# The order of the products inside a weight chunk: output tile outside, contraction step inside

## The chip, the cores and the metric

The kernel runs on one core of a Trainium2 chip. The metric is the device time of one execution in microseconds; the median of three runs is given. The profile is of one further execution of the same program.

## The reference

Two transformer-like blocks are applied one after the other to 256 tokens of width 2048, in float32. The first takes the tokens through a conditioned norm, a projection to four parts (a state space mixer and dilated attention), an output projection and a gated feed-forward network. The second puts 16 meta tokens ahead of them and applies a feed-forward network, a projection, a pooling mixer and forget-gate attention, an output projection and a third feed-forward network. Cut to the part that matters here, which is the dense products:

```python
proj = h @ w_in                      # 2048 x 4096
y = y * sigmoid(y @ w_glu)           # 1024 x 1024
x = x + gate1 * (mixed @ w_out)      # 2048 x 2048
x = x + gate2 * ((silu(h2 @ w_gate) * (h2 @ w_up)) @ w_down)   # hidden 5632
# the second block: the same kinds of product again,
# h + 0.5 * swiglu(...), u @ w_in_2, mix @ w_out_2, h + 0.5 * swiglu(...)
```

## The kernel before, in words

**Tiling.** Everything lies transposed: features on the 128 partitions, tokens along the free dimension (256 tokens, or 272 with the meta tokens). A weight matrix is read in chunks of 512 rows by 512 columns, 1 MB each, as a tile of 128 partitions x 4 contraction steps (CK = 4) x 512 columns. A chunk feeds four output tiles of 128 features, m = 0 to 3. A group is the chunks that accumulate into the same four output tiles, 4 of them in most stages (cpg), 2 or 3 in a few.

**Precision.** Each float32 product is made of three: the weights are split into a high and a low part, and so are the activations. TensorE computes high weight x high activation (L540), high weight x low activation (L541) and low weight x high activation (L542). So a chunk is 4 steps x 4 tiles x 3 = 48 products, each with a load of 128 x 128 weights ahead of it.

**Order of the work.** SyncE issues the loads into a ring of four raw buffers (`stream`, L388) and waits for the user of the buffer four chunks before. ScalarE splits off the high part into one of two buffers (`split_hi`, L404) when the products of the chunk two before are done (chunk_done). VectorE computes the low part (`split_lo`, L409) and signals lo_ready. TensorE runs `products`: for each chunk it waits once for the group's four PSUM banks if it is the group's first (bank_free), for the activations where they are new, and for lo_ready, and then issues the 48 products. The last of them signals chunk_done. Between chunks VectorE and ScalarE also empty the PSUM banks of the finished group (L742, L796 and others), and there are two sets of four banks, so that one is filled while the other is emptied.

**Where tiles lie.** `out_tile` (above `products`) gives each of the four output tiles a PSUM bank of its own, in the half that the group has. Only in w_in do two tiles of 256 columns share a bank (m // 2), and there only the even tile's first product has the start flag.

**Who calls it.** `products` is used for all dense stages: w_in (with the pieces of the state space mixer between the chunks, `beside`), glu, w_out, the up and down parts of the three feed-forward networks (`ffn_pe`), w_in_2 and w_out_2. There are 496 chunks. Elsewhere, at L1898, the forget gate of the second block is computed with 48 products from weights of 8 columns, all into one tile:

```python
for k in range(KT):
    for w, x in ((wf_hi, act_hi), (wf_hi, act_lo), (wf_lo, act_hi)):
        mm = pe.matmul(ps[0:HEADS, 4, 0:T], w[:, k, :], x[:, k, :], ...
```

Of the kernel before, what the change touches and what calls it, by code (L numbers as in the profile page):

```python
# [35 lines left out]
CK = 4  # L36
# [110 lines left out]
def build(nc, a, out):  # L147
# [4 lines left out]
    with stack:  # L152
# [197 lines left out]
        def loop(eng, start, end, body):  # L350

            if end - start == 1:
                body(start)
            elif end > start:
                with eng.Fori(start, end) as i:
                    body(i)
# [140 lines left out]
        def group_index(p, it, g):  # L497

            return 1 + p.g0 // 2 + g // 2 + it * (p.groups // 2)
# [9 lines left out]
        def out_tile(name, half, m, n):  # L509

            if name == "w_in":
                return ps[:, 2 * half + m // 2, n * (m % 2):n * (m % 2) + n]
            return ps[:, 4 * half + m, 0:n]

        def products(pe, name, hi, lo, cols, ready, norm=None, beside=None):
            p = byname[name]
            n = cols.stop - cols.start
            shared = name == "w_in"

            def body(it, norm=None):  # L520
                for j in range(p.per["S"]):
                    g, c = divmod(j, p.cpg)
                    half = g % 2
                    if norm and j == 3:
                        norm_pe(pe, norm, 4)
                    if norm and j == 4:
                        pe.wait_ge(ms_ready, NORMS.index(norm) + 1)
                    if beside:
                        beside(it * p.per["S"] + j)
                    if c == 0:  # L530
                        pe.wait_ge(bank_free[half], group_index(p, it, g))
                    if ready(c) is not None:
                        pe.wait_ge(*ready(c))
                    pe.wait_ge(lo_ready, p.before["S"] + it * p.per["S"] + j + 1)
                    for t in range(CK):
                        k = CK * c + t
                        for m in range(4):
                            o = out_tile(name, half, m, n)
                            whi, wlo = w_hi[j % 2][:, t, P * m:P * m + P], w_lo[j % 2][:, t, P * m:P * m + P]
                            pe.matmul(o, whi, hi[:, k, cols], start=(k == 0 and not (shared and m % 2)), stop=False)  # L540
                            pe.matmul(o, whi, lo[:, k, cols], start=False, stop=False)  # L541
                            mm = pe.matmul(o, wlo, hi[:, k, cols], start=False, stop=(k == CK * p.cpg - 1 and not (shared and m % 2 == 0)))  # L542
                    mm.then_inc(chunk_done, 1)

            if norm:
                body(0, norm)
            for it in range(p.iters if beside else 0):
                body(it)
            loop(pe, 1 if norm else p.iters if beside else 0, p.iters, body)


# [11 lines left out]
        def norm_pe(pe, name, bank_=0):  # L563

            i = NORMS.index(name)
            for g in range(QUADS):
                pe.wait_ge(ssq_ready, QUADS * i + g + 1)
                mm = pe.matmul(ps[:, bank_, 0:T], ones, ssq[:, g, :], start=(g == 0), stop=(g == QUADS - 1))  # L568
            mm.then_inc(ssq_sum, 1)
# [1421 lines left out]
```

## Time and profile before

| | |
|---|---|
| median of 3 runs | 3419.1 us (3419.04 to 3423.09) |
| profiled execution, its own time | 3418.91 us |
| its span, first to last instruction | 3416.8 us |
| mean granted TensorE clock | 0.944 of full speed |
| TensorE products busy | 3190.7 us, 93% |
| VectorE busy | 1925.2 us, 56% |
| ScalarE busy | 1209.9 us, 35% |
| GpSimd busy | 198.0 us, 6% |
| read from HBM | 626.16 MB, mean 184 GB/s |

A matmul's row in the timeline has its start and its duration. Successive matmuls overlap, so the spacing of their starts, and not the duration, says how fast TensorE goes. PE is TensorE's matmuls, PEld its weight loads, DVE is VectorE, ACT ScalarE, POOL GpSimd, SP SyncE; q behind a name is that engine's queue of instructions. ps is the tile of all eight PSUM banks.

### The profile page before, as it was taken

The numbers are of one execution on the slowest core, as the hardware profiler recorded it, in microseconds if no ns is written. First come the engines' busy times: TensorE is split into PE (matmuls) and PEld (weight loads), VectorE is DVE, ScalarE is ACT, GpSimd is POOL, SyncE is SP. The second block draws the span as 40 slices with busy tenths as digits, with TensorE's granted clock in tenths as the row PEclk, the third lists the DMA queues.
The fourth block names the chain that finished last, engine by engine and source line by source line (L and its number), as shares of the span: only waits on it lengthen the run. The fifth ranks groups of instructions, "written<-read, shape, count | busy, mean of one in ns | idle before, by whom it ended". The sixth has DMA issues, their size and how long they took to land. (4 is left out here: it accounts for less than half of the span.)

```text
span 3416.8 us, 57672 instructions
## 1 busy us (share of the span) xinstructions
PE 3190.7 (93%) x25282; PEld 3105.7 (91%) x25282; DVE 1925.2 (56%) x1800; ACT 1209.9 (35%) x1067; POOL 198.0 (6%) x194
## 2 busy tenths in 40 slices
PE   3499758799999999999999999999899999999999
PEld 3499648799999999999999999999659999999999
DVE  7888597867444444654445445654335554455454
ACT  2264423333233333433333333433324433333333
POOL 3434120000000000000000000021000000000000
PEclk6699859899999999999999999999859999999999
DMA  9765357577555555555555555588205555555553
GB/s 328 243 204 191 129 185 271 210 270 268 174 185 185 188 189 187 185 170 177 173 173 172 178 175 176 173 173 171 79 1 178 181 187 188 182 191 187 185 184 136
DMA packets 328689, 630.26 MB, mean 184 GB/s; under 512 B 22452, under 2 KB 24008, under 8 KB 328280
## 3 DMA queue, kind: packets, MB, share of 16 engines
q1 hardware_dynamic: 317512, 624.79, 55.6%
q10 hardware_dynamic: 11040, 3.51, 0.5%
q8 instruction: 103, 1.69, 0.2%
q14 instruction: 34, 0.28, 0.0%
HBM read 626.16 MB, written 2.10 MB: 184 GB/s over the span
## 5 line engine op out<-in xcount | busy, mean ns | idle before, releaser
L409 DVE TENSOR_TENSOR w_lo<-raw,w_hi 128x2048 fp32r<-128x2048 f32 x496 | 1139.6, 2298 | 1266.7 <-ACT w_hi L404 1266.5
L404 ACT ACTIVATE w_hi<-raw 128x2048 fp32r<-128x2048 f32 x496 | 949.8, 1915 | 1803.5 <-PE ps L542 1755.1
L540 PE MATMUL ps<-act_hi,w_hi 128*128 128x256 f32 (+1 forms) x5056 | 1440.4, 285 | 48.8 <-DVE w_lo L409 28.8
L541 PE MATMUL ps<-act_lo,w_hi 128*128 128x256 f32 (+1 forms) x5056 | 1438.8, 285 | 0.0
L542 PE MATMUL ps<-act_hi,w_lo 128*128 128x256 f32 (+1 forms) x5056 | 1436.5, 284 | 0.0
L540 PEld LDWEIGHTS ps<-act_hi,w_hi 128*128 128x128 f32 x5056 | 959.1, 190 | 52.6 <-issue 26.4
L541 PEld LDWEIGHTS ps<-act_lo,w_hi 128*128 128x128 f32 x5056 | 958.2, 190 | 0.1
L542 PEld LDWEIGHTS ps<-act_hi,w_lo 128*128 128x128 f32 x5056 | 957.7, 189 | 0.0
L540 PE MATMUL ps<-hid_hi,w_hi 128*128 128x256 f32 (+1 forms) x2880 | 814.8, 283 | 12.7 <-DVE w_lo L409 8.2
L542 PE MATMUL ps<-hid_hi,w_lo 128*128 128x256 f32 (+1 forms) x2880 | 812.9, 282 | 0.0
L541 PE MATMUL ps<-hid_lo,w_hi 128*128 128x256 f32 (+1 forms) x2816 | 795.5, 283 | 0.0
L540 PEld LDWEIGHTS ps<-hid_hi,w_hi 128*128 128x128 f32 x2880 | 544.0, 189 | 14.2 <-issue 13.0
L542 PEld LDWEIGHTS ps<-hid_hi,w_lo 128*128 128x128 f32 x2880 | 543.6, 189 | 0.0
L541 PEld LDWEIGHTS ps<-hid_lo,w_hi 128*128 128x128 f32 x2816 | 530.8, 189 | 0.0
L1830 POOL TENSOR_TENSOR win<-proj 128x542 f32<-128x542 f32 x4 | 6.3, 1573 | 1838.7 <-DVE proj L702 1838.5
L423 DVE SCALAR_TENSOR_TENSOR acc<-raw,cond,acc 128x512 f32 (+1 forms) x120 | 94.8, 790 | 5.1 <-DMA raw<-in_w_ada 0.3
L423 DVE SCALAR_TENSOR_TENSOR accg<-raw,cond,accg 128x512 f32<-128x512 f32 (+1 forms) x120 | 92.9, 774 | 3.5
L428 PE MATMUL ps<-const,acc 128*128 128x1 f32 x64 | 14.3, 351 | 43.6 <-DVE acc L423 43.6
L428 PEld LDWEIGHTS ps<-const,acc 128*128 128x128 f32 x64 | 14.1, 330 | 44.0 <-DVE acc L423 44.0
L1552 PE MATMUL ps<-const,pn 128*128 128x128 f32 (+1 forms) x64 | 22.0, 447 | 32.0 <-DVE pn L1658 31.9
L796 DVE SCALAR_TENSOR_TENSOR res<-ps,res 128x256 f32<-128x256 f32 (+1 forms) x112 | 40.3, 422 | 19.3 <-PE ps L542 19.3
L742 ACT ACTIVATE sig<-sig 128x1088 f32<-128x1088 f32 (+1 forms) x22 | 23.9, 1087 | 75.1 <-DVE sig L760 75.1
(285 smaller groups left out, 1607.8 us busy)
## 6 DMA issues: line engine op xcount, KB each, us to landing
raw<-in_w_ada SPq DMA_DIRECT2D x96, 1024.0 KB, 5.1
raw<-in_ffn_w_gate SPq DMA_DIRECT2D x88, 1024.0 KB, 5.0
raw<-in_ffn_w_up SPq DMA_DIRECT2D x88, 1024.0 KB, 5.0
raw<-in_ffn_w_down SPq DMA_DIRECT2D x88, 1024.0 KB, 5.0
raw<-in_w_in SPq DMA_DIRECT2D x64, 1024.0 KB, 5.9
raw<-in_w_ffn_gate SPq DMA_DIRECT2D x44, 1024.0 KB, 5.1
raw<-in_w_ffn_up SPq DMA_DIRECT2D x44, 1024.0 KB, 5.1
raw<-in_w_ffn_down SPq DMA_DIRECT2D x44, 1024.0 KB, 5.0
```

The costliest lines, as they stand in the source:

```text
L404: act.activation(w_hi[b][:, :, :], raw[j % RING][:, :, :], ACT.Copy).then_inc(hi_ready, 1)
L409: dve.tensor_tensor(w_lo[b][:, :, :], raw[j % RING][:, :, :], w_hi[b][:, :, :].bitcast(F32), ALU.subtract).then_inc(lo_ready, 1)
L423: dve.scalar_tensor_tensor(out=acc, in0=w, scalar=x, in1=acc, op0=ALU.mult, op1=ALU.add).then_inc(acc_step, 1)
L428: mm = pe.matmul(ps[:, bank_, col + m:col + m + 1], acc[:, P * m:P * m + P], ones[:, 0:1], start=True, stop=True, skip_group_check=True)
L540: pe.matmul(o, whi, hi[:, k, cols], start=(k == 0 and not (shared and m % 2)), stop=False)
L541: pe.matmul(o, whi, lo[:, k, cols], start=False, stop=False)
L542: mm = pe.matmul(o, wlo, hi[:, k, cols], start=False, stop=(k == CK * p.cpg - 1 and not (shared and m % 2 == 0)))
L742: act.activation(sig[:, :, 0:n], sig[:, :, 0:n], ACT.Silu).then_inc(sig_ready, 1)
L796: ins = dve.scalar_tensor_tensor(out=r, in0=ps[:, 4 * (g % 2) + m, 0:n], scalar=s, in1=r, op0=ALU.mult, op1=ALU.add)
L1552: mm = pe.transpose(ps[0:r, 2 + u % 2, P * k:P * k + P], pn[:, u % 2, cols], ident)
L1830: link(pool, "pool", pool.tensor_tensor(dst[:, :, w - 1:T], src[:, :, w - 1:T], src[:, :, w // 2 - 1:T - w // 2], ALU.add))
```

## The change

In `products`, the loop over the four output tiles goes outside and the loop over the four contraction steps of the chunk inside. In the kernel before, all four tiles are served for a step before the next step comes. Afterwards all twelve products of one tile (four steps of three) follow one another, and then come those of the next tile. The flags, waits and signals are the same expressions as before.

```diff
                     pe.wait_ge(lo_ready, p.before["S"] + it * p.per["S"] + j + 1)
-                    for t in range(CK):
-                        k = CK * c + t
-                        for m in range(4):
-                            o = out_tile(name, half, m, n)
+                    for m in range(4):
+                        o = out_tile(name, half, m, n)
+                        for t in range(CK):
+                            k = CK * c + t
                             whi, wlo = w_hi[j % 2][:, t, P * m:P * m + P], w_lo[j % 2][:, t, P * m:P * m + P]
                             pe.matmul(o, whi, hi[:, k, cols], start=(k == 0 and not (shared and m % 2)), stop=False)
                             pe.matmul(o, whi, lo[:, k, cols], start=False, stop=False)
```

## Rows read from the trace of the kernel before

**Rows 1.** The overview: busy time by engine, granted clock in 40 slices.
```profile
PE 3190.7 (93%) x25282; PEld 3105.7 (91%) x25282; DVE 1925.2 (56%) x1800; ACT 1209.9 (35%) x1067; POOL 198.0 (6%) x194
...
PEclk6699859899999999999999999999859999999999
```

**Rows 2.** Windows, TensorE alone: window, length, busy (instructions), clock, DMA share, GB/s.
```profile
514.00:889.60 375.60, 340.97 (x2760) 0.95 0.70 246
889.60:1386.00 496.40, 496.40 (x4222) 1.00 0.55 186
1530.00:2200.00 670.00, 670.00 (x5345) 1.00 0.52 175
2555.00:3411.00 856.00, 848.28 (x7153) 0.99 0.53 177
```

**Rows 3.** Costliest groups by line: count | busy us, mean ns | idle before, releaser.
```profile
L409 DVE TENSOR_TENSOR w_lo<-raw,w_hi 128x2048 fp32r<-128x2048 f32 x496 | 1139.6, 2298 | 1266.7 <-ACT w_hi L404 1266.5
...
L540 PE MATMUL ps<-act_hi,w_hi 128*128 128x256 f32 (+1 forms) x5056 | 1440.4, 285 | 48.8 <-DVE w_lo L409 28.8
L541 PE MATMUL ps<-act_lo,w_hi 128*128 128x256 f32 (+1 forms) x5056 | 1438.8, 285 | 0.0
L542 PE MATMUL ps<-act_hi,w_lo 128*128 128x256 f32 (+1 forms) x5056 | 1436.5, 284 | 0.0
...
L540 PE MATMUL ps<-hid_hi,w_hi 128*128 128x256 f32 (+1 forms) x2880 | 814.8, 283 | 12.7 <-DVE w_lo L409 8.2
L542 PE MATMUL ps<-hid_hi,w_lo 128*128 128x256 f32 (+1 forms) x2880 | 812.9, 282 | 0.0
L541 PE MATMUL ps<-hid_lo,w_hi 128*128 128x256 f32 (+1 forms) x2816 | 795.5, 283 | 0.0
```

**Rows 4.** Waits, who for whom: us in total, times, longest.
```profile
SPq L388 <- DVE w_lo L409: 2490.4, 491, 18.0
...
ACT w_hi L404 <- PE ps L542: 1755.1, 459, 13.7
...
PE ps L540 <- DVE w_lo L409: 37.0, 12, 8.2
```

**Rows 5.** Timeline of a steady 272-column chunk, TensorE: start us, duration us, instruction.
```profile
1529.87 0.28 PE L540 MATMUL ps<-act_hi,w_hi 128*128 128x272 f32 x1
1529.99 0.30 PE L541 MATMUL ps<-act_lo,w_hi 128*128 128x272 f32 x1
1530.12 0.29 PE L542 MATMUL ps<-act_hi,w_lo 128*128 128x272 f32 x1
1530.25 0.28 PE L540 MATMUL ps<-act_hi,w_hi 128*128 128x272 f32 x1
...
1530.62 0.28 PE L540 MATMUL ps<-act_hi,w_hi 128*128 128x272 f32 x1
...
1530.99 0.29 PE L540 MATMUL ps<-act_hi,w_hi 128*128 128x272 f32 x1
...
1531.38 0.29 PE L540 MATMUL ps<-act_hi,w_hi 128*128 128x272 f32 x1
```

**Rows 6.** Timeline of the forget-gate products at L1898, 28th last and last.
```profile
2429.16 0.29 PE L1898 MATMUL ps<-act_hi,wf_lo 128*8 128x272 f32 x1
...
2432.54 0.29 PE L1898 MATMUL ps<-act_hi,wf_lo 128*8 128x272 f32 x1
```

**Rows 7.** Timeline of the first GLU chunk, clock still at its lower level, nine steps.
```profile
515.02 0.41 PE L540 MATMUL ps<-hid_hi,w_hi 128*128 128x256 f32 x1
...
516.94 0.41 PE L540 MATMUL ps<-hid_hi,w_hi 128*128 128x256 f32 x1
```

## The prediction

> **What bounds the kernel now.** I read the overview first: TensorE is busy for 3190.7 of 3416.8 us, VectorE for 56% and ScalarE for 35%, and the granted clock is at nine tenths or more almost everywhere in the dense stages [rows 1]. Busy time alone does not say that an engine is at its pace, so the second view was the table of windows [rows 2]. In two long stretches of feed-forward work TensorE is busy for the whole window, 496.40 of 496.40 us and 670.00 of 670.00 us, at a granted clock of 1.00, which is the 2.4 GHz level. The DMA share there is 0.55 and 0.52. Between them these two kinds of stretch are most of the program; the last feed-forward network is 848.28 of 856.00 us.
>
> The groups by line [rows 3] give the number of products: 3 x 5056 + 2 x 2880 + 2816 = 23,744. The program has 496 weight chunks (L409 ran 496 times) of 48 products, 23,808 in all; the missing 64 are the low products of the GLU stage, whose operand is a slice of hid_hi and which stand in a smaller group. The waits [rows 4] then show who is early and who is late: ScalarE's split of the next chunk waits for the last product of a chunk (1755.1 us in 459 waits), the loads wait for VectorE's low half (2490.4 us), while TensorE waits for that low half only 12 times, 37.0 us in all. So the whole pipeline hangs on TensorE, and in a steady stretch no wait is left to remove. What counts is the spacing of one product after another.
>
> **The spacing.** From the windows: 496.40 us / 4220 = 117.6 ns for 256 columns and 670.00 / 5343 = 125.4 ns for 272 columns (two products of each count began ahead of the window's edge and are left out). At 1.2 GHz the same product takes 1.92 us / 9 = 213 ns [rows 7].
>
> **What the change does, part by part.** It removes and adds no instruction. Each chunk keeps 48 products and 48 weight loads, the wait for the banks, the wait for the activations and the wait for the low half all stand ahead of the loops, and the signal chunk_done stays on the 48th product, which is t=3, m=3 in both orders. So ScalarE, VectorE and the load queue see the same events at the same places: no DMA is moved, no queue is passed, no wait is added. That tile 0 is complete some us earlier in the last chunk of a group is worth nothing, because nobody is told before the 48th product. Price of all this: 0, and the cover is not needed, since none of it is made later.
>
> What does move is the address that follows an address. Today a product goes to another output tile (in all stages but w_in another PSUM bank) 16 times a chunk, the step into the next chunk included; afterwards 4 times. That is 12 x 496 = 5952 tile changes fewer. In return, the moving rows change 16 times a chunk where they changed 4 times: 5952 more such changes.
>
> Two views price this. First, a dense chunk [rows 5]: from 1529.87 to 1531.38 us three products take 0.38, 0.37, 0.37 and 0.39 us. The first three of these spans end in a change of tile with the same moving rows, the last one in a change of tile and of k; steps inside a tile are 0.12 and 0.13 us. A change of tile is not to be seen above the 0.01 us of the view. Second, and decisive for me, the forget-gate products at L1898 [rows 6]: they are 48 products of 272 columns into one tile of one bank, k innermost, new moving rows after every third. That is the new order exactly, except that their weights have 8 columns where dense ones have 128. Once the clock is up they go from 2429.16 to 2432.54 us in 27 steps: 125.2 ns each, against 125.4 ns in the dense stretch.
>
> So if the dense products took the pace of that group, the gain would be 0.2 ns x 23,808 = 5 us; the view's rounding (0.01 us over 27 steps, 0.37 ns) leaves room for 8.8 us either way. I take a quarter of the 5 us, because only 12 of the 48 predecessors in a chunk become others: -1.2 us. Bounds: -8.8 and +8.8 us. The products at 1.2 GHz are equally spaced too [rows 7], and nothing is gained there.
>
> The sum: the profiled execution took 3418.91 us (span 3416.8 and 2.1 around it), minus 1.2 is 3417.7; the median of the three runs is 0.2 above the profiled one, so **3418 us**. A measurement of this kernel can tell about 0.2%, 6.8 us, from no change, and this is well inside it.
>
> **Rivals.** (a) *Faster: the rotation through the banks costs something that is spread over all products.* All dense spacings are above the columns at 2.4 GHz: 117.6 against 106.7 ns, where at 1.2 GHz 213 ns is just 256 columns. If a tile change caused part of that and the queue smeared it over its neighbours, fewer changes would help. With 5 ns a change (half a unit of the view) it is 30 us, 3389 us; it decides from 1.15 ns a change (6.8 us / 5952). Against it: the group of rows 6 has no tile change at all and keeps the same excess (125.2 against 113.3 ns). The Trainium skill, "TensorE: Matmul & The Clock Gate", section "A second HAM failure mode: psum-queue depth-cycling", says that cycling through PSUM banks makes TensorE idle briefly between groups so that its clock falls back; by that rule this change should gain. The trace does not agree here: in the steady windows there is no idle time and the clock is 1.00 [rows 2]. The same page, section "Wait — 56ns, not 53.3ns?", gives N / 2.4 GHz plus 2.5 ns as spacing; at that pace the dense products would take 8.4 and 9.6 ns less each, some 209 us as an estimate, and the group of rows 6, which is in the new order, does not reach it either. Chance of (a): 0.08.
>
> (b) *Slower: a long run into one tile backs up.* Today two of three products add onto the result of the one before; afterwards 11 of 12. If the fourth and later ones of a run had to wait for the sums ahead of them, 9 of every 12 products (17,856) would pay. With 5 ns each (a step of 0.13 instead of 0.125 us) it is 89 us, 3508 us; it decides from 0.38 ns a product. For it: rows 6 write only 8 of 128 partitions, so a full-width run of more than three is nowhere in this trace. Against it: the second and third products of today's triples are no later than the first. Chance 0.05.
>
> (c) *It does not do what it says in w_in.* There two tiles share a bank and only the first product of the pair clears it, so the bank is held for 24 products rather than one tile for 12. This is 32 chunks of 496, and there TensorE has other waits. Time as forecast, within a microsecond; 0.02.
>
> **How the numbers follow.** Forecast and (c) together 0.87; (a) 0.08, (b) 0.05. The forecast's own bounds are 3418 - 8.8 and 3418 + 8.8, and their outer edge is the rounding of one view, so 3410 to 3426 holds nearly all of it and the weak ends of (a) and (b). Both rivals in full lie outside, together about 0.1.
>
> **What would show it right or wrong.** In the changed profile the two steady windows (they may start a few us elsewhere) should again be wholly busy with 117.6 and 125.4 ns a product, and a chunk should last 5.65 and 6.02 us. The waits for the last product of a chunk should be 1755 us within some 10 us. Successive products should show the same 0.12 and 0.13 us steps in the first, fourth and twelfth place of a tile's run. Rival (a) shows as a chunk shorter than 5.63 us, (b) as steps of 0.13 us or more from the fourth product of a run on, with L542 longest waited for. If the time moves by over 7 us while the spacing stays, my list of what is untouched was wrong, and the waits of TensorE and its clock in the short cold stretches would be the place to look.

## The result and the profile after

The changed kernel takes 3434.28 us (median of six runs, 3433.03 to 3436.18) against 3421.23 us before (six runs, 3419.04 to 3423.57). The ratio is 1.0039, with a 95% interval of 1.0026 to 1.0051: slower, by some 13 us. The forecast was 3418 us, 3410 to 3426.

The overview line of the changed kernel answers to [rows 1]; its span is 3433.3 us against 3416.8:

```profile
PE 3210.1 (93%) x25282; PEld 3125.2 (91%) x25282; DVE 1925.0 (56%) x1800; ACT 1209.7 (35%) x1067; POOL 193.3 (6%) x194
```

The instructions are the same in number, and TensorE is busy for 19 us more. The windows of [rows 2] again, now of the changed kernel (window, length, TensorE busy with count, clock, DMA share, GB/s):

```profile
514.00:889.60 375.60, 337.44 (x2716) 0.94 0.70 244
889.60:1386.00 496.40, 496.40 (x4197) 1.00 0.55 186
1530.00:2200.00 670.00, 670.00 (x5315) 1.00 0.51 173
2555.00:3411.00 856.00, 848.46 (x7056) 0.98 0.53 177
```

The two steady windows are as fully busy as before, at the same clock, and hold fewer products: 4197 for 4222 and 5315 for 5345. With the two that began ahead of the window left out, 496.40 / 4195 = 118.3 ns a product where it was 117.6, and 670.00 / 5313 = 126.1 where it was 125.4. So TensorE's own spacing grew by 0.7 ns a product, 0.033 us a chunk. The waits, which answer to [rows 4], did not come from elsewhere:

```profile
SPq L388 <- DVE w_lo L409: 2507.3, 491, 18.4
...
ACT w_hi L404 <- PE ps L542: 1774.6, 460, 13.8
...
PE ps L540 <- DVE w_lo L409: 34.6, 12, 8.2
```

TensorE waits no longer for VectorE than before (34.6 us for 37.0). ScalarE waits 20 us longer for TensorE, and the loads, which wait for the low half that comes after ScalarE's split, wait 17 us longer.

Where in a chunk does it go? These are rows of the timeline of one steady 256-column chunk of the first feed-forward network in the kernel before: its products 1, 13, 25, 30 and 37 and the first of the next chunk (start us, duration us):

```profile
957.41 0.28 PE L540 MATMUL ps<-act_hi,w_hi 128*128 128x256 f32 x1
...
958.83 0.28 PE L540 MATMUL ps<-act_hi,w_hi 128*128 128x256 f32 x1
...
960.25 0.28 PE L540 MATMUL ps<-act_hi,w_hi 128*128 128x256 f32 x1
...
960.84 0.28 PE L542 MATMUL ps<-act_hi,w_lo 128*128 128x256 f32 x1
...
961.63 0.28 PE L540 MATMUL ps<-act_hi,w_hi 128*128 128x256 f32 x1
...
963.05 0.28 PE L540 MATMUL ps<-act_hi,w_hi 128*128 128x256 f32 x1
```

Twelve products are one contraction step t here. Steps 0, 1 and 3 take 1.42 us each, step 2 takes 1.38. The gain sits in its last seven spacings: 960.84 to 961.63 is 0.79 / 7 = 113 ns. The same five places in a chunk of the changed kernel, which are now spread over tiles:

```profile
962.98 0.28 PE L540 MATMUL ps<-act_hi,w_hi 128*128 128x256 f32 x1
...
964.40 0.28 PE L540 MATMUL ps<-act_hi,w_hi 128*128 128x256 f32 x1
...
965.82 0.28 PE L540 MATMUL ps<-act_hi,w_hi 128*128 128x256 f32 x1
...
966.41 0.28 PE L542 MATMUL ps<-act_hi,w_lo 128*128 128x256 f32 x1
...
967.24 0.28 PE L540 MATMUL ps<-act_hi,w_hi 128*128 128x256 f32 x1
...
968.66 0.28 PE L540 MATMUL ps<-act_hi,w_hi 128*128 128x256 f32 x1
```

All four quarters take 1.42 us, the seven spacings 0.83 / 7 = 119 ns, and the chunk 5.68 us instead of 5.65. The run of 113 ns is gone. In the trace every steady chunk of a width repeats its kernel's picture place by place, in all stages.

By stages: 5.3 of the 16.5 us of span stand ahead of the first GLU product (519.59 us after the start for 514.24; w_in and the first attention, with a mean clock of 0.83 for 0.85 between them), 7.0 from there to the first product of w_out_2, and 4.2 in the rest. The first 5.3 can't be put down to the order: the traces of the experiments below have that product at 517.08 and 516.68 us with the steady chunk of before (e2, e8) and at 516.62 and 517.62 us with that of the changed kernel (e3, e9). What belongs to the chunks is the 11.2 us behind it. The 464 chunks behind w_in would give 464 x 0.033 = 15 us if all were steady; the rest is presumably absorbed where TensorE waits anyway.

### The profile page after: what moved, and what is told of

Read it like the earlier page. It is cut to its first block and busy times, and to the rows that moved or that the text cites. A ratio compares the mean times of both kernels' runs of the same rounds, so it can differ in the third digit from the quotient of the medians.

```text
span 3433.3 us, 57672 instructions
## 1 busy us (share of the span) xinstructions
PE 3210.1 (93%) x25282; PEld 3125.2 (91%) x25282; DVE 1925.0 (56%) x1800; ACT 1209.7 (35%) x1067; POOL 193.3 (6%) x194
## 5 line engine op out<-in xcount | busy, mean ns | idle before, releaser
L404 ACT ACTIVATE w_hi<-raw 128x2048 fp32r<-128x2048 f32 x496 | 949.8, 1915 | 1817.0 <-PE ps L542 1774.6
```

The costliest lines, as they stand in the source:

```text
L404: act.activation(w_hi[b][:, :, :], raw[j % RING][:, :, :], ACT.Copy).then_inc(hi_ready, 1)
```

## The experiments

Activation rows are 272 x 4 = 1088 bytes apart, which is 4 x 256 + 64. So the four rows that a chunk uses start at four different places within 256 bytes, and four rows on the same four places come again. "Place" below means this. A step is a contraction step t, and a row is the moving row of that step. The diffs are cut to the lines that matter, and some are paraphrased; e1 to e4 and e7 to e10 were executed once each, so they are read from their traces, where the length of a steady chunk repeats to 0.001 us or two.

**One row for all products (e1).** Theory R (the spacing depends on the place of the moving row) against theory T (a long run into one tile is slow) and W (the jump to another weight row is slow).

```diff
+r = CK * c + row     # row by stage: up0 0, up1 1, up2 2, down0 3, down1 0, down2 1, others 3
-pe.matmul(o, whi, hi[:, k, cols], ...)
+pe.matmul(o, whi, hi[:, r, cols], ...)
```

> The changed kernel with one edit: all 48 products of a chunk read one of its four activation rows, row 0 in up0 and down1, row 1 in up1 and down2, row 2 in up2, row 3 in down0 and in all other stages (so three of four contraction steps use the wrong activations and the output is not the reference's). In the third network (ffn3) the products also stand in the order of the kernel before. Weights, output tiles, waits and counts are unchanged. Activation rows start 1088 bytes apart, 4 x 256 + 64, so the four rows of a chunk start at four places within 256 bytes, the same four in every chunk. Theory R (rows): TensorE's spacing depends on where the moving row starts, and after a change of row it takes about five products to settle; the kernel before stays 12 products on a row and settles (113.3 ns in row 2, seen in its trace), the changed one only 3 and never does. R expects, at 256 columns, a chunk of 5.65 us with row 0, 5.69 with row 1, 5.44 with row 2 and 5.76 with row 3, in both orders alike; at 272 columns 6.03 to 6.08 with rows 0 to 2 and 5.92 with row 3. Theory T (tile): long runs of additions into one output tile are slow; it expects 5.68 us in ffn1 whatever the row, and 5.647 in ffn3. Theory W (weights): the jump to another weight row after every third product is slow; it expects the same as T.

Measured: 3426.35 us. TensorE in windows of down0 (row 3), up1 (row 1), down1 (row 0) and up2 (row 2) of ffn1, all in the changed order and at 256 columns:

```profile
875.00:960.00 85.00, 85.00 (x710) 1.00 0.49 162
970.00:1140.00 170.00, 170.00 (x1435) 1.00 0.55 185
1150.00:1235.00 85.00, 85.00 (x725) 1.00 0.55 186
1240.00:1365.00 125.00, 125.00 (x1106) 1.00 0.58 192
```

With two products off each count the spacings are 120.1 ns (row 3), 118.6 (row 1), 117.6 (row 0) and 113.2 (row 2). Four stages of one network that differ in the row differ by 6%, and the expected chunks are met: 5.76, 5.69, 5.65 and 5.44 us. At 272 columns, ffn2's up0 (row 0), down0 (3), up1 (1) and up2 (2):

```profile
1500.00:1620.00 120.00, 120.00 (x960) 1.00 0.53 175
1635.00:1722.00 87.00, 87.00 (x708) 1.00 0.53 176
1730.00:1915.00 185.00, 185.00 (x1463) 1.00 0.52 171
2020.00:2160.00 140.00, 140.00 (x1107) 1.00 0.52 173
```

That is 125.3, 123.2, 126.6 and 126.7 ns (row 0 a little under what was expected, 125.3 x 48 = 6.01 us a chunk for 6.03). T and W expected one figure for all. One thing did not fit. In ffn3, three chunks with row 0 took 5.44 us, not 5.65, and nine with row 2 took 5.65 us, not 5.44. So 117.8 and 113.3 ns can both be had with either of these rows, and the place alone does not decide between them. More on that below.

**A new tile with every product (e2).**

```diff
 for t in range(CK):
+    for kind in range(3):
         for m in range(4):
-            three products
+            the product of this kind
```

> The kernel before with one edit: inside a contraction step t, the four tiles' L540 products come first, then the four L541, then the four L542, so the output tile changes with every product (48 times a chunk instead of 16) while the moving row's place within 256 bytes still changes 4 times. Nothing is left out. R (rows) expects a chunk as in the kernel before, 5.647 us at 256 columns and 6.020 at 272, within 0.02 us, and a time of 3419 to 3424 us. T (tile) expects that fewer additions in a row are faster: from 16 to 4 tile changes cost 0.033 us a chunk, so 16 to 48 should gain about 0.09 us a chunk, 5.56 us, 44 us in all. W (weights) expects a small loss or nothing, since the weight row changes as often as before.

Measured: 3421.56 us, the kernel before beside it 3419.82. Windows of 256 and 272 columns:

```profile
900.00:1380.00 480.00, 480.00 (x4083) 1.00 0.56 186
1530.00:2200.00 670.00, 670.00 (x5344) 1.00 0.52 174
```

The kernel before has x5345 in the second. In the first, the kernel before and the changed one have

```profile
900.00:1380.00 480.00, 480.00 (x4083) 1.00 0.55 186
```

```profile
900.00:1380.00 480.00, 480.00 (x4059) 1.00 0.55 185
```

Three times as many tile changes alter nothing, which R expected and T did not. This bears also on the rule that I had set beside rival (a), that cycling through PSUM banks makes TensorE idle between groups and its clock fall back (the Trainium skill, "TensorE: Matmul & The Clock Gate", section "A second HAM failure mode: psum-queue depth-cycling"): with 48 changes of bank a chunk there is no idle time in these windows and the clock is 1.00. No run here shows that failure.

**One weight row (e3).**

```diff
-whi, wlo = w_hi[j % 2][:, t, ...], w_lo[j % 2][:, t, ...]
+whi, wlo = w_hi[j % 2][:, 0, ...], w_lo[j % 2][:, 0, ...]
```

> The changed kernel with one edit: every product takes its weights from row 0 of the chunk (t = 0) instead of its own row t, so within a tile the weight address only alternates between the high and the low buffer (three of four contraction steps use the wrong weights; the output is not the reference's). Moving rows, tiles and order are those of the changed kernel. R (rows) and T (tile) expect the changed kernel's chunk, 5.680 us at 256 columns and 6.053 at 272, and no change of the total beyond 0.1%. W (weights) expects the kernel before's chunk, 5.647 us and 6.020.

Measured: 3434.33 us, the changed kernel's time, and 900 to 1380 us holds the changed kernel's 4059 products:

```profile
900.00:1380.00 480.00, 480.00 (x4059) 1.00 0.55 186
```

W, which expected the chunk of before, is excluded.

**Moving the rows by 64 bytes (e4), and moving the weights by 64 bytes (e8).** Both are made on the kernel before.

```diff
+cursor[0] += 64     # e4: ahead of act_hi and all behind it
+cursor[0] += 64     # e8: ahead of w_hi, and 192 more behind w_lo
```

> The kernel before with one edit: act_hi and everything laid out behind it (act_lo, hid_hi, hid_lo and more) start 64 bytes later. Nothing is left out, the order is that of the kernel before. R (rows) expects the spacings to move by one contraction step: the run of 113.3 ns that the kernel before shows in the last seven products of step t = 2 appears in step t = 1, and the spacing of 120 ns at the end of t = 3 appears in t = 2; the chunk as a whole stays at 5.65 us within 0.03. T and W expect the same picture as in the kernel before, with the 113.3 ns in t = 2, since neither the tiles nor the weights move.

> The kernel before with one edit: the four split weight buffers (w_hi, w_lo) start 64 bytes later, and all that lies behind them 256 bytes later, so the moving rows keep their place within 256 bytes. Nothing is left out. Theory R-absolute: only the moving row's own place counts; the picture of the kernel before stays (113.3 ns at the end of step t = 2, chunk 5.647 us). Theory R-relative: the distance between the moving row and the weights within 256 bytes counts; the run of 113.3 ns moves to step t = 3, since the row of that step now has the distance that row 2 had. In both the total stays within 0.2%.

Measured: 3419.06 and 3423.30 us, the 256-column chunk 5.647 us in both. The timeline of e4, products 18 and 25 of a chunk that starts at 957.15 us:

```profile
959.16 0.28 PE L543 MATMUL ps<-act_hi,w_lo 128*128 128x256 f32 x1
...
959.96 0.28 PE L541 MATMUL ps<-act_hi,w_hi 128*128 128x256 f32 x1
```

and of e8, product 42 and the first of the next chunk, in a chunk that starts at 962.61 us:

```profile
967.46 0.28 PE L544 MATMUL ps<-act_hi,w_lo 128*128 128x256 f32 x1
...
968.25 0.28 PE L542 MATMUL ps<-act_hi,w_hi 128*128 128x256 f32 x1
```

Seven spacings take 0.80 us in step 1 of e4 and 0.79 us in step 3 of e8; the fast run has moved from step 2 to step 1 and to step 3, as R-relative said. So neither the row's number nor its place alone counts, but the distance between the moving row's place and the weights' place.

The weight slices all start at one place, since they lie 2048 bytes apart from step to step and 512 from tile to tile. At 256 columns the moving slice begins 64 bytes into its row, behind the 16 meta tokens. Counted from the weights' place, row 2 at 256 columns and row 3 at 272 are thus both 192 bytes on, and these were the fastest rows of the two widths in e1.

The distance does not tell everything. At 272 columns the short step of e4 has moved too, but its chunk is 6.033 us, where the kernel before and e8 have 6.020. The same distances in the same order gave two lengths, and no run shows why.

**Rows changing as in the changed kernel, tiles as in the kernel before (e9).** This is the direct separation.

```diff
+for i in range(4 * CK):
+    t, m = i % 4, (i + i // 4) % 4
```

> The 16 pairs of output tile and contraction step are gone through on a diagonal: step t = i mod 4 and tile m = (i + i // 4) mod 4 for i = 0 to 15, three products each. Nothing is left out. So the moving rows follow one another exactly as in the changed kernel (t = 0, 1, 2, 3, 0, 1, ...; 16 changes a chunk), while the output tile changes after every third product, as in the kernel before (16 tile changes). Theory R (rows, now: the distance between moving row and weights within 256 bytes, and the order in which the distances come) expects the changed kernel's chunk, 5.680 us at 256 columns and 6.053 at 272, to within 0.003. Theory T (tile) expects the kernel before's, 5.647 and 6.020.

Measured: 3435.30 us, the kernel before 3419.38 (median of nine).

```profile
900.00:1380.00 480.00, 480.00 (x4059) 1.00 0.57 186
1530.00:2200.00 670.00, 670.00 (x5315) 1.00 0.53 173
```

These are the changed kernel's counts, and the spacings agree with its place by place, within 1 ns in the two chunks compared. The twelve additions in a row into one tile have no part in the loss; the order of the moving rows has all of it.

**The same number of changes in another order (e10).**

```diff
-for t in range(CK):
+for t in (0, 2, 1, 3):
```

> The changed kernel with one edit: inside a tile the contraction steps come in the order t = 0, 2, 1, 3. Nothing is left out. Tiles, the length of a run into one tile (12) and the number of row changes (16) are those of the changed kernel. The run with tiles in pairs had 8 changes and was faster (5.613 us) than the kernel before with 4 (5.647), so the number of changes alone sets nothing. R in its present form, that the sequence of distances sets the chunk, expects a chunk that differs from 5.680 us by more than 0.005, in either direction, and from 6.053 at 272 columns; it has no figure for it. The counting form of R, a fixed price for a change, and T (tile) both expect 5.680 and 6.053 unchanged.

Measured: 3435.42 us.

```profile
900.00:1380.00 480.00, 480.00 (x4059) 1.00 0.57 185
1530.00:2200.00 670.00, 670.00 (x5327) 1.00 0.53 174
```

Half a miss. At 272 columns the chunk is 6.040 us instead of 6.053, as the sequence form of R said; at 256 columns the single spacings change but their sum stays 5.680, which it had not expected.

**Tiles in pairs: six products on a row (e7, and again as e11).**

```diff
+for t2 in range(2 * CK):
+    t = t2 % CK
+    for m in (2 * (t2 // CK), 2 * (t2 // CK) + 1):
```

> An order halfway between the two: the tiles are taken in pairs (m = 0 and 1, then 2 and 3), and inside a pair the contraction steps t = 0 to 3 are gone through, two tiles each. Nothing is left out. A chunk has 8 changes of moving row, where the kernel before has 4 and the changed one 16; the longest stay on a row is 6 products. Theory R (rows) after the first four runs: the settled chunk is the mean of the four fixed-row chunks, (5.653 + 5.694 + 5.440 + 5.760) / 4 = 5.637 us at 256 columns, and each change of row costs 2.5 to 2.7 ns over that (5.647 with 4 changes, 5.680 with 16). R expects 5.637 + 8 x 0.0027 = 5.658 us within 0.006, and 6.02 to 6.04 us at 272 columns. T (tile) expects the middle by additions in a row (16, 8, 4 tile changes), also near 5.66, and is already excluded by the run with a new tile for every product; this run measures R's dose.

> The order with tiles in pairs again, as in e7_two_tiles, now timed in rounds. Its steady chunk was 5.613 us at 256 columns and 6.000 at 272, against 5.647 and 6.020 in the kernel before. On 332 and 164 chunks that is 11.3 + 3.3 = 14.6 us if every chunk were steady; the one look showed 8 us. Expected ratio to the kernel before 0.996 to 0.998. If the one look was chance and the chunks' gain is given back in waits, the ratio is 1.000.

Measured: 3410.66 us in one execution beside 3418.61, and 3407.43 us as the median of five, ratio 0.9961 (0.9948 to 0.9975). My 5.658 us for the chunk was wrong and in the wrong direction: it is 5.613 us, and 6.000 at 272 columns. The windows of the second run:

```profile
900.00:1380.00 480.00, 480.00 (x4107) 1.00 0.58 188
1530.00:2200.00 670.00, 670.00 (x5363) 1.00 0.54 176
```

So 12, 6 and 3 products on a row give 5.647, 5.613 and 5.680 us. There is no fixed price for a change of row.

**All rows at one place, in both orders (e5 and e6).** Nothing is left out; only the layout of the activations in the stages that use 256 columns changes.

```diff
+act2_hi = at("act2_hi", [P, KT, SEQ], F32R, offset=act_at + 192)
+act2_lo = at("act2_lo", [P, KT, SEQ], F32R, offset=act_at + 17408 + 192)
+hid2_hi = at("hid2_hi", [P, KT, SEQ], F32R, offset=hid_at + 192)
+hid2_lo = at("hid2_lo", [P, KT, SEQ], F32R, offset=hid_at + 17408 + 192)
 ... (w_in, ffn1 and ffn3 write and read these)
```

> The order of the kernel before, nothing left out. In w_in and in the first and third feed-forward network (ffn1, ffn3), where 256 tokens are used, the activations (high and low) and the hidden activations are kept in rows of 256 columns, 1024 bytes apart, that all start at the place within 256 bytes that row 2 has in the kernel before; the 16 meta columns are not copied there. w_out, glu, w_out_2, ffn2 and w_in_2 keep their rows of 272. R (rows) expects every steady chunk of ffn1 and ffn3 at 5.44 us (the fixed-row run's figure for that place) instead of 5.647: 0.207 us x 264 chunks = 55 us, and up to 7 us more in w_in's 32 chunks, so 3358 to 3366 us. Rival N: the fixed-row runs were fast because the same row was read again and again, not because of its place; then a chunk stays at 5.65 us and the time at 3419.

> The same rows as in the kernel e5_one_place (256 columns, all at one place within 256 bytes, in w_in, ffn1 and ffn3), but in the order of the changed kernel, with a new moving row after every third product. Nothing is left out. R (rows) says that a change of row costs only if the place within 256 bytes changes: 5.44 us a chunk in ffn1 and ffn3 too, and a time above e5_one_place only by the other stages' share, 0.033 us x about 200 chunks = 6 to 7 us. Rival C: every change of row costs 2.7 ns, whatever its place; then a chunk has 16 x 0.0027 = 0.043 us more than 5.44, 5.48 us, and the time is about 16 us above e5_one_place.

Measured: 3382.70 us, ratio 0.9892 (0.9875 to 0.9908), in the order before, and 3383.43 us, ratio 0.9893 (0.9876 to 0.9909), in the changed order. ffn1 between 900 and 1380 us in each:

```profile
900.00:1380.00 480.00, 480.00 (x4238) 1.00 0.59 194
```

```profile
900.00:1380.00 480.00, 480.00 (x4238) 1.00 0.59 193
```

480 / 4236 = 113.3 ns in both: with one place the order is of no account in these steady chunks, and rivals N and C are out. In the traces e6's span is 6.7 us longer than e5's, as expected for the stages that keep rows of 272; the medians of four, 0.7 us apart, are too scattered to show it (3379 to 3390 us in e6). The gain of 36 us is only about two thirds of what I expected, though. By the traces ffn1 gained 26 of the 27 us expected of it, ffn3 only 9 of 27, and w_in next to nothing. In ffn3, 75 of the 132 chunks of e5 end at 117.8 ns a product, that is 5.65 us a chunk and not 5.44, and so do 75 of e6. The windows of e5 in ffn3's down0, early in up1, and a little later in up1:

```profile
2815.00:2895.00 80.00, 80.00 (x681) 1.00 0.55 184
2905.00:2950.00 45.00, 45.00 (x384) 1.00 0.58 187
2964.00:2979.00 15.00, 15.00 (x135) 1.00 0.60 203
```

80 / 679 = 117.8 ns, 45 / 382 = 117.8, then 15 / 133 = 112.8 (a whole chunk there is 5.440 us, 113.3 ns). Between the second and the third window stand these rows of the timeline, TensorE's first and then VectorE's:

```profile
2957.54 0.28 PE L546 MATMUL ps<-hid_hi,w_lo 128*128 128x256 f32 x1
2957.74 0.38 PE L544 MATMUL ps<-hid_hi,w_hi 128*128 128x256 f32 x1
```

```profile
2955.40 2.28 DVE L413 TENSOR_TENSOR w_lo<-raw,w_hi 128x2048 fp32r<-128x2048 f32 x1
```

The low half is ready at 2957.68, and so the first product of that chunk starts 0.20 us after its predecessor, 0.08 us late. From its third product on the spacing is 113 ns, until the next such delay, behind the product at 2979.62, puts it back to 118. With the place constant, TensorE kept one of at least two cadences, and a delay of under 0.1 us could change it, though not every one did: in e1's ffn3 a product came 0.09 us late and the next chunk stayed at 117.8 ns. The chunks of ffn3 that did not fit in the run with one row change behind delays of the same kind.

**Both together (e12).**

```diff
+(the rows of e5_one_place)
+for m in (2 * (t2 // CK), 2 * (t2 // CK) + 1):
```

> The rows of e5_one_place (256 columns, one place, in w_in, ffn1 and ffn3) together with the order of e7_two_tiles in all stages. Nothing is left out. Where rows share one place the order did not matter (5.440 us in ffn1 in both orders), so a gain over e5_one_place is expected only in the stages that keep rows of 272: 164 chunks x 0.020 + 36 x 0.034 = 4.5 us, so 3375 to 3380 us, ratio 0.987 to 0.989. If one place and order interact, ffn1's chunk is no longer 5.440 us.

Measured: 3379.47 us, ratio 0.9880 (0.9865 to 0.9895), as expected: ffn1's chunk is 5.440 us, save for six of up0 at 5.65 in the other cadence, and the 272-column one is 6.000. This is the lowest median here; its interval overlaps that of e5_one_place, so that it is faster than e5 is carried by the 272-column chunks of the trace and not by the times.

## Why the prediction was wrong

- **What bounds the kernel.** Right. The steady windows had no wait, behind the first GLU product the changed kernel moved the time by the spacing, and nobody else became late.
- **Nothing added, nothing moved in the queues and waits.** Right: the same counts, TensorE's wait for the low half 34.6 us for 37.0. That ScalarE's wait for TensorE grew from 1755.1 to 1774.6 us, where I had allowed 10, follows from the spacing.
- **"A change of tile is not to be seen".** Right, and shown: 48 changes a chunk instead of 16 cost nothing, and 4 instead of 16 gain nothing.
- **The step that failed** is the pricing of the other half of the move, the 5952 more changes of moving row. I named them, and then priced both halves with the forget-gate products of [rows 6] as "the new order exactly, except that their weights have 8 columns". The term came out as -1.2 us; it is +11.2 us in the trace behind the first GLU product, and the medians differ by +13. In those products the weights too start elsewhere at each step, 32 bytes on, so their distances to the moving rows are not those of the dense ones. After the experiments that is enough to make them a bad stand-in; that it is the reason they keep 125.2 ns is only argued. Nor are they evenly spaced: in the trace of before, their last 27 spacings run through 127, 128, 126, 120, 124 and 125 ns over and over, so that 125.2 was the mean of a pattern too.
- **The share that changes.** I took a quarter because "only 12 of the 48 predecessors in a chunk become others". That is the number of tile changes that go away. The first products of 15 of the 16 groups of three get another predecessor. In a term of 5 us this is of no weight.
- **The chunk was read too short.** [Rows 5] hold the 12 products of one contraction step of a 272-column chunk and the first of the next. The rows of a whole 256-column chunk, in the trace of before, show seven spacings of 113 ns in one step and none in the others. Identical instructions with two spacings were a hint that the spacing depends on what is addressed, and so that a new order of addresses could not be costed by a mean.
- **The bounds.** They came from the rounding of one view (8.8 us over all products), not from a spread between rows. With 113 ns for some products and 120 for others, the bound should have been several ns a product; the range of 3410 to 3426 was too narrow by that.
- **Rival (a)**, a cost of rotating through banks: excluded. It set out from the excess over the columns, and part of that excess does hang on an order, but on that of the rows and not of the tiles. The best cadence seen is 113.3 ns for 256 columns. By the Trainium skill's formula ("TensorE: Matmul & The Clock Gate", section "Wait — 56ns, not 53.3ns?") it would be 109.2 ns as an estimate, and no run reached it.
- **Rival (b)**, slower because of long runs into one tile: it had the sign but not the cause. A full-width run of twelve with rows at one place keeps 113.3 ns, and with tiles changing after every third product the loss is all there.
- **Rival (c)** shows nowhere: the shortest chunk of w_in is 5.685 us for 5.647, much the step that the other stages made.

What is shown: the loss comes from the order in which the moving rows' places, against the weights' place, follow one another. With that order and the old order of tiles it is all there (e9), with one weight row it stays (e3), and with all rows at one place the same change costs ffn1's steady chunks nothing (e6 beside e5). What stays open is the mechanism inside TensorE or its reads, why six products on a row are better than twelve and three worse, why e4's 272-column chunk is longer, and why some delays change the cadence and others don't. None of the runs can tell.

## What to carry to other kernels

Where TensorE is busy without a gap, print the start-to-start spacing of one whole steady period product by product before reordering it: if equal instructions have several spacings, the order and the layout can be worth up to a per cent or so, as here, and neither can be costed from an average. Then lay the moving rows out so that they all start at the place, relative to the weights, that shows the shortest spacing; here 1024 bytes of pitch instead of 1088 in three stages gained 1.1%, where the order alone gave from -0.4% to +0.4%. Repeat the measurement after any change of layout, since 64 bytes more ahead of a buffer move the picture to other products, and read every stage: one layout kept 113.3 ns in ffn1 and, for 75 of 132 chunks, 117.8 ns in ffn3.

## What the runs showed of the hardware

- With 128x128 weights, 256 moving float32r columns and one row for all, the spacing in ffn1 at the 2.4 GHz level was 113.2, 117.6, 118.6 or 120.1 ns, by the place of the row within 256 bytes; with 272 columns in ffn2 it was 123.2, 125.3, 126.6 or 126.7. In ffn3 two of the four rows were seen at both 113.3 and 117.8 ns.
- In both widths the fastest row of e1 was the one 192 bytes past the weights' place (113.2 and 123.2 ns).
- At 256 columns the picture moved when the rows did (64 bytes on: one step earlier) and when the weights did (64 bytes on: one step later), the chunk staying 5.647 us.
- At a constant place the 256-column spacing stayed at 113.3 or at 117.8 ns for tens of chunks, and in e5 changed after a product had come 0.08 us late.
- Changing the output tile and PSUM bank with every product cost nothing measurable: 4083 products in 480 us in e2 and in the kernel before.
